# Splitting v of both PEER layers into bf16 halves beside the heads of the first mixer, and forming the expert outputs from the halves

## The reference

```python
    def block(args):
        xb, ib, gb = args
        hb = jax.nn.gelu(jnp.einsum('tkd,td->tk', u[ib], xb), approximate=False)
        return jnp.einsum('tk,tkd->td', gb * hb, v[ib])
```

## Time and profile before

| | us |
|---|---|
| median of 3 runs (lowest, highest) | 4829.14 (4827.85, 4833.03) |
| the profiled execution, its own time | 4834.75 |
| its span, first to last instruction | 4833.2 |

### The profile page before, as it was taken

The page is one execution under the profiler, slowest core; times in us unless marked ns, Lnnn a source line. Parts: engine busy times, 40 slices in busy tenths (PEclk is TensorE's granted clock), DMA queues, the critical chain, the costliest instruction groups (busy, mean ns, idle before and its releaser), DMA issues. The chain is left out here.

```text
span 4833.2 us, 54964 instructions
## 1 busy us (share of the span) xinstructions
PE 4347.5 (90%) x19374; PEld 2496.9 (52%) x19374; DVE 3212.7 (66%) x6400; ACT 1013.2 (21%) x1581; POOL 720.5 (15%) x548
## 2 busy tenths in 40 slices
PE   8999998978979989999998877987878998999998
PEld 5767674645545545544444555554444554444443
DVE  1666642679978767765653675469997886766664
ACT  2111101122224431100001253213333441100000
POOL 0000000002221113232210000001221112332220
PEclk9999999989989999999999999999998999999999
DMA  4111131149877779999992000116776779999995
GB/s 146 39 39 44 37 133 55 55 182 350 324 278 267 294 275 375 370 385 394 384 360 70 31 1 31 47 50 242 282 284 234 284 272 353 364 397 400 400 396 196
DMA packets 291813, 1101.75 MB, mean 228 GB/s; under 512 B 30704, under 2 KB 131184, under 8 KB 222576
## 3 DMA queue, kind: packets, MB, share of 16 engines
q0 software_dynamic: 74752, 539.00, 28.3%
q1 hardware_dynamic: 185136, 470.64, 27.2%
q10 hardware_dynamic: 31680, 88.88, 4.8%
HBM read 1005.61 MB, written 92.80 MB: 227 GB/s over the span
## 5 line engine op out<-in xcount | busy, mean ns | idle before, releaser
L774 POOL DMA_INDIRECT room_p<-in_uv,ga_eidx_p x512 | 702.8, 1373 | 3309.5 <-DVEq L801 2105.0
L1324 PE MATMUL ex_psF_p<-ex_vst_p,ex_gh_p 128*128 128x512 f32 x1920 | 851.5, 599 | 34.3 <-DVE ex_gh_p L1405 18.1
L800 DVE SCALAR_TENSOR_TENSOR ga_acc_p<-room_p,ga_gw_p,ga_acc_p 128x1024 f32<-128x1024 f32 x504 | 625.1, 1282 | 21.8 <-issue 1.7
L1324 PEld LDWEIGHTS ex_psF_p<-ex_vst_p,ex_gh_p 128*128 128x128 f32 x1920 | 365.9, 192 | 482.5 <-issue 460.6
L786 DVE CUSTOM_DVE_ANT_0 room_p<-room_p,hx_p 128x1024 f32<-128x1024 f32 x512 | 605.5, 1220 | 4.0 <-issue 4.0
L891 PE MATMUL eh_psH_sl_p<-h_hi_p,eh_uhi_sl_p 128*128 128x384 bf16 x1056 | 367.6, 348 | 160.0 <-DVE eh_ulo_sl_p L855 159.9
L1324 PE MATMUL ex_psF_p<-ex_ust_p,ex_gh_p 128*128 128x512 f32 x1152 | 502.1, 593 | 6.6 <-DVE ex_gh_p L1405 6.5
L1405 DVE TENSOR_TENSOR ex_gh_p<-ex_est_p,ex_gst_p 128x384 f32<-128x384 f32 x196 | 107.3, 558 | 397.7 <-DMA ex_est_p<-hidden 253.3
L891 PE MATMUL eh_psH_sl_p<-h_lo_p,eh_uhi_sl_p 128*128 128x384 bf16 x1056 | 366.3, 347 | 0.0
L1324 PEld LDWEIGHTS ex_psF_p<-ex_ust_p,ex_gh_p 128*128 128x128 f32 x1152 | 217.7, 190 | 286.6 <-issue 285.4
L891 PE MATMUL eh_psH_sl_p<-h_hi_p,eh_ulo_sl_p 128*128 128x384 bf16 x1056 | 365.4, 346 | 0.0
(11 more groups left out here) (248 smaller groups left out, 6275.5 us busy)
## 6 DMA issues: line engine op xcount, KB each, us to landing
ex_vst_p<-in_uv SPq DMA_DIRECT2D x160, 512.0 KB, 8.4
eh_ust_sl_p<-in_uT SPq DMA_DIRECT2D x132, 512.0 KB, 5.4
gates<-gt_gs_p ACTq DMA_DIRECT2D x24, 2048.0 KB, 8.0
ex_gst_p<-gates SPq DMA_DIRECT2D x128, 384.0 KB, 13.0
ex_ust_p<-in_uv SPq DMA_DIRECT2D x96, 512.0 KB, 9.3
ex_est_p<-hidden SPq DMA_DIRECT2D x196, 192.0 KB, 10.2
eh_ust_gt_p<-in_uT SPq DMA_DIRECT2D x64, 512.0 KB, 6.6
ex_ust_p<-in_uT SPq DMA_DIRECT2D x60, 512.0 KB, 8.8
```

Of the source, the lines that this page charges most:

```text
L774: self.nc.gpsimd.indirect_dma_start(self.slot[s % self.RING], None, self.uv, bass.IndirectOffsetOnAxis(self.eidx[:, s:s + 1], 0)).then_inc ...
L800: nc.vector.scalar_tensor_tensor(acc[:], row, self.gw[:, s:s + 1], acc[:], op0=ALU.mult, op1=ALU.add)
L1324: last = nc.tensor.matmul(psF[:, t, x, :], gh[n % 3][:, P * t:P * t + P], vbuf[vslot[n]][:, BANK * x:BANK * x + BANK], start=(n == 0), sto ...
```

## The change

In the first mixer, 32 blocks (`VSPLIT`) are handled beside each head, 16 of layer 0 and 16 of layer 1, so 256 in all, which is all of v. A block is 128 experts by 1024. POOL loads it in f32 (512 KB) into one of two buffers `vraw`; ScalarE copies it to bf16 (`high`), in four groups of eight ahead of the evacuations of the next head's projections, and for the last head four ahead of each of the eight modulation groups; VectorE subtracts that to get the low half (`low`), two blocks behind each of the 16 steps; POOL stores both halves together (512 KB) to a DRAM tensor `halves` and then issues the load after next. The two buffers of each kind are freed by the store's completion (`v_free`) and by the low half (`v_low`).

In both expert stages v is loaded as the two halves, into the same buffers and with as many bytes. The gated values are split as well, on ScalarE (`high`) and VectorE (`low`), with four buffers of each half, and a tile's output is formed from three bf16 products: high by high, high by low, low by high. The two row buffers of the modulation become one.

```diff
@@ rec_mixer
+        vraw = [sb(f"rec_vraw{i}", [P, D]) for i in range(2)]
+        vhl = [sb(f"rec_vhl{i}", [P, 2, D], BF16) for i in range(2)]
...
+            def fetch(h, j):
+                pool.dma_start(vraw[j % 2][:], rows_in[j // 16][h, j % 16, :, D:2 * D]).then_inc(v_in[j % 2], 16)
+
+            def stored(h, j):
+                pool.wait_ge(v_out[j % 2], 16 * (VSPLIT // 2 * h + j // 2) + 16)
+                pool.sem_inc(v_free, 1)
+
+            def split_rows(h, nxt):
+                for j in range(VSPLIT):
+                    pool.wait_ge(v_low, VSPLIT * h + j + 1)
+                    pool.sem_inc(v_seen, 1)
+                    pool.dma_start(halves[j // 16][h, j % 16], vhl[j % 2][:]).then_inc(v_out[j % 2], 16)
+                    if j + 2 < VSPLIT:
+                        fetch(h, j + 2)
+                    elif nxt is not None:
+                        fetch(nxt, j + 2 - VSPLIT)
+                    if j > 0:
+                        stored(h, j - 1)
+                stored(h, VSPLIT - 1)
+
             load(0)
+            fetch(0, 0)
+            fetch(0, 1)
             with pool.Fori(1, RH) as h:
+                split_rows(h - 1, h)
                 store(h - 1)
...
+            def high(h, js):
+                for j in js:
+                    act.wait_ge(v_in[j % 2], 16 * (VSPLIT // 2 * h + j // 2) + 16)
+                    act.wait_ge(v_free, VSPLIT * h + j + 1)
+                    nc.scalar.activation(vhl[j % 2][:, 0, :], vraw[j % 2][:], ACT.Copy).then_inc(v_high, 1)
...
-                evacuate(h, s, [Q_, FF_, FB_, G_])
+                for n in (Q_, FF_, FB_, G_):
+                    high(h - 1, range(VSPLIT * n // 4, VSPLIT * (n + 1) // 4))
+                    evacuate(h, s, [n])
...
             for g in range(later.groups):
+                high(RH - 1, range(VSPLIT * g // later.groups, VSPLIT * (g + 1) // later.groups))
...
+            def low(h, n):
+                for j in range(VSPLIT * (n - 1) // 16, VSPLIT * n // 16):
+                    dve.wait_ge(v_high, VSPLIT * h + j + 1)
+                    nc.vector.tensor_tensor(vhl[j % 2][:, 1, :], vraw[j % 2][:], vhl[j % 2][:, 0, :],
+                                            ALU.subtract).then_inc(v_low, 1)
...
                     take(h, n - 1)
+                    low(h, n)
@@ peer_experts
+        GH = 4 if halves is not None else 3
...
+                if halves is not None:
+                    sp.dma_start(vbuf[vslot[n]].bitcast(BF16), halves[n]).then_inc(v_in[vslot[n]], 16)
...
+            def output_halves(n):
+                pe.wait_ge(v_in[vslot[n]], 16 * vturn[n] + 16)
+                pe.wait_ge(g_low, n + 1)
+                both = vbuf[vslot[n]].bitcast(BF16)
+                for t in range(ND):
+                    tok = slice(P * t, P * t + P)
+                    for j, (g, v0) in enumerate(((g_hi[n % GH], 0), (g_hi[n % GH], D), (g_lo[n % GH], 0))):
+                        for x in range(2):
+                            last = nc.tensor.matmul(psF[:, t, x, :], g[:, tok], both[:, v0 + BANK * x:v0 + BANK * x + BANK],
+                                                    start=(n == 0 and j == 0), stop=(n == NK - 1 and j == 2))
+                last.then_inc(added, 1)
...
+            def high(n):
+                act.wait_ge(gated, n + 1)
+                if n >= GH:
+                    act.wait_ge(added, n - GH + 1)
+                nc.scalar.activation(g_hi[n % GH][:], gh[n % 3][:], ACT.Copy).then_inc(g_high, 1)
+
             for n in range(NK):
+                if halves is not None:
+                    high(n)
                 gelu(n + 1)
...
+            def low(n):
+                dve.wait_ge(g_high, n + 1)
+                nc.vector.tensor_tensor(g_lo[n % GH][:], gh[n % 3][:], g_hi[n % GH][:], ALU.subtract).then_inc(g_low, 1)
...
                 if n >= 3:
-                    dve.wait_ge(added, n - 2)
+                    dve.wait_ge(added if halves is None else g_low, n - 2)
...
                 take_u(n + 3)
+                while halves is not None and lows < (n + 1 if n < late or n == NK - 1 else n):
+                    low(lows)
+                    lows += 1
@@ kernel
+        halves = [nc.dram_tensor(f"halves{l}", [RH, 16, P, 2, D], BF16, kind="Internal").ap() for l in range(2)]
```

More of the change, by code:

```diff
@@ L222, in rec_mixer @@
         adab = sb("rec_adab", [P, NMOD * KD, 2])
-        rows = [sb(f"rec_rows{i}", [2, 2, BANK]) for i in range(2)]
+        rows = sb("rec_rows", [2, 2, BANK])
         wst = sb("rec_wst", [P, 5, KD, P])
@@ L568, in head @@
                 for d in range(2):
+                    low(h, 15 + d)
                     n = TR0 + d
@@ L1218, in _, with peer_experts @@
                 sp.wait_ge(sv[s], 16 * (NBL // 2))
-def peer_experts(nc, cst, modT, uT, uv, gates, hid, gather, late, h_hi, h_lo, tag):
+def peer_experts(nc, cst, modT, uT, uv, halves, gates, hid, gather, late, h_hi, h_lo, tag):
     J, TB = 8, 32
@@ L1317, in hidden @@
                 hidden_products(nc, psH[:, n % 2, 0:TD], u_hi[n % 3], u_lo[n % 3], h_hi, h_lo).then_inc(made, 1)
+            def output_halves(n):
[9 more added lines that the diff above has]
+                last.then_inc(added, 1)
             def output(n):
+                if halves is not None:
+                    return output_halves(n)
                 pe.wait_ge(v_in[vslot[n]], 16 * vturn[n] + 16)
@@ L1422, in _, with peer @@
             dve.drain()
-def peer(nc, cst, modT, wqk, uT, uv, gates, hid, tag, ada=None):
+def peer(nc, cst, modT, wqk, uT, uv, halves, gates, hid, tag, ada=None):
     tiles, pairs = (60, (2, 2, 3)) if ada else (72, (2, 1, 3))
@@ L1440, in peer @@
         peer_gates(nc, cst, pk, gates, gather, (uT, h_hi, h_lo, hid, late + tiles), tag)
-        peer_experts(nc, cst, modT, uT, uv, gates, hid, gather, late, h_hi, h_lo, tag)
+        peer_experts(nc, cst, modT, uT, uv, halves, gates, hid, gather, late, h_hi, h_lo, tag)
 NQ, NKV = AH * HD // P, AKV * HD // P
@@ L1845, in _ @@
             runs(dve, one)
+VSPLIT = 32
 class Const:
@@ L1865, in program @@
         cst.normw = normw[0]
+        halves = [nc.dram_tensor(f"halves{l}", [RH, 16, P, 2, D], BF16, kind="Internal").ap() for l in range(2)]
+        by_block = [v.rearrange("h j p e d -> (h j) p (e d)") for v in halves]
         with ExitStack() as c1:
@@ L1870, in program @@
                       {"cond": a["cond"], "xT": a["xT"], "ident": a["ident"], "iota": a["iota"], "normw": a["normw"],
-                       "normw_sb": normw})
+                       "normw_sb": normw},
+                      [a[f"uv{l}"].rearrange("(h j p) d -> h j p d", p=P, j=16) for l in range(2)], halves)
             out_projection(nc, cst, a["rec_w_out"], yT, mods[0], "_rec")
```

22 lines of the change are left out of this document (16 added, 6 removed).

## The result

| us | before | after |
|---|---|---|
| median (4 runs each) | 4830.32 | 5593.99 |
| lowest, highest | 4827.85, 4833.03 | 5583.95, 5604.63 |
| span of the profiled execution | 4833.2 | 5596.1 |

The changed kernel takes 1.1581 times as long, 95% interval 1.1557 to 1.1605: 764 us more. Forecast were 5266 and a range up to 5450, so the sign was right and the size too small: 437 us of the 764.

The account below looks back on a forecast made before the run. It took TensorE to bound the mixer, and TensorE and DMA together the expert stages. The profiled 4834.75 + 502 - 65 = 5272, stated as 5266 us for the median; forecast 5110 to 5400, range 5090 to 5450.

Parts of the forecast that it names:

- Term 2: First mixer: splitting v beside the heads lengthens their steps, +502 us, bounds +388 to +754.
- ring of 7.5: Mixer: store issue, next load, its landing, high half and low half follow in a closed loop, 7.5 us a step.
- rival A: Mixer: store, load and weights meet in the queues, loop 8.6 to 9.6 us, total 5400 to 5520; chance 0.15.
- VectorE's floor: Mixer: VectorE's own work plus two subtractions make a step at least 4.90 us.
- Term 1: Expert stages: bf16 output matmuls spare TensorE time, but bytes stay; -65 us, bounds -20 to -105.
- the DMA ceiling: Expert stages: transfers go no faster than 405 GB/s, so a late tile's 1.97 MB take 4.86 us.
- the new wait: Expert stages: TensorE's output waits for the gated values' low half, up to 0.3 us on 60 early tiles, 18 us.
- B: Mixer: TensorE falls to its lower clock, +124 us, total 5390; chance 0.10.
- C: Mixer: transfers are hidden, VectorE bounds steps of 4.9 to 5.8 us, total 4955 to 5065; chance 0.12.
- D: Expert stages: 405 GB/s is no limit, they gain 320 us; mixer steps fall to 4.9, total 4699; chance 0.02.
- The signs it gave: Mixer: steps 7.5 us, landing 4 to 4.5, DMA about 280 GB/s; expert stages some 45 and 20 us shorter.
- would make it wrong: Mixer steps near 5 us, an expert stage shorter by over 100 us, or stages that grow by the new wait.

Follow-up runs that it names:

- all three edits: Only the bf16 expert stages, against the kernel before: low half ahead of u's, at once in late tiles, awaited only before the last 6 matmuls; -24.9 us, ratio 0.9952.

## Why the prediction was wrong

**Term 2, the mixer: right in kind, mis-sized (+502 forecast, +740 measured).** The waits are those it named, VectorE's for ScalarE and, for three quarters of it, ScalarE's for the load. Its ring of 7.5 was 9.0 in a plain step and 9.36 over a head. Two terms were too small. The load, from the start of its issue: 0.55 + 3.3 + 0.75 = 4.60 forecast, 5.28 measured; POOL's wake: "some 0.1 for the semaphore", 0.76 measured. The first was short by more than it looks: the row's 3.3 runs from the start of an issue, so the forecast counted the load's 0.55 twice, and the landing itself, 3.3 + 0.75, was 1.2 too low. The rest lies in the first interval of a head, 12.7 where 7.5 was taken for it as for the others, and in the last head, whose step is 10.7. The step that failed is the choice inside the bounds: 5.4 for the landing was there, with +754, and was set aside "because 5.4 was measured beside gathers of 1 MB", and rival A because of "12% load in the mixer before". But the load that counts is the one after the change, and the change itself brings it to a DMA share of 0.66 to 0.69. Only the store ahead on the same queue was priced; the run with the stores on SyncE's queue shows that the place on the queue was not it.

**What stood behind the ring was not named.** Where the load is taken out (four buffers), the release through POOL is next, at 8.4, then the store's landing, at 8.1. The forecast listed the store's completion as freeing a buffer, but did not follow it through POOL's list, where it stands behind the next store and load.

**VectorE's floor** was near: 4.90 forecast, 5.18 measured without transfers, +190 against +229.

**Term 1, the expert stages: the DMA ceiling was right, the new wait was mis-sized (-65 forecast, +25 in the changed kernel).** With the low half formed at once the late tiles give 37 and 23 us, 60 together, where the forecast had 22 + 19 and 19, also 60. That is not luck alone: with all three edits stage 1's late tiles run at the ceiling while gathers last, 384 us for 80 tiles or 4.8 each at 403 GB/s, where 4.86 was forecast.

```profile
2122.00:2506.00 384.00, 325.58 (x1398) 138.23 (x1399) 281.31 (x435) 48.84 (x118) 92.14 (x80) 0.95 1.03 403
```

The step that failed is the bound of the wait, "up to 0.3 us on 60 tiles, 18 us of the 38", with the sentence that the small splits "lie beside the DMA time". The low half cost 39 us in the early tiles and held back 39 in the late ones, where it was not looked for. In the early tiles the forecast took VectorE as 23 to 28 of 40 us busy and left out its wait for ScalarE; with it, VectorE's list was as long as the tile, and its new operation came on top. In the late tiles the low half was priced by the operation's length, and in an in-order list it costs what stands ahead: the next tile's load (up to 10.84).

**Rivals.** A is what happened in the mixer, with a step in its range of 8.6 to 9.6; its 5400 to 5520 still carried the -65, so the 5594 lies above it. B's clock came (0.78), but its price did not: some 4 us at the heads' ends, and in the steps TensorE was not waited for. C needed transfers that land a microsecond sooner; they landed two later. D is refuted: with all three edits TensorE has gaps in the late tiles at 404 and 406 GB/s, and half the gathers' bytes make these tiles shorter.

**The signs it gave.** Steps of COPY_PREDICATED at 7.5: 9.4 in the mean. Landing 4 to 4.5: 5.3. DMA 280 GB/s: 217. Expert stages 45 and 20 shorter: 5 shorter and 23 longer by the table above. Of what "would make it wrong" it had the last: stages that grow by the new wait.

## What to carry to other kernels

Price a transfer's landing at the load of the DMA engines that the change makes, not the one it finds, and for a ring of few buffers take it from a row measured beside as much traffic. A new small operation costs what stands ahead of it in its engine's order, waits for loads included, so place it and the consumer's wait before pricing it. Count an engine's waits for its own helpers as part of its list: VectorE was busy for 26.8 of 40 us and yet had no room. Where a wait is removed, follow the buffer's release instruction by instruction: the next chain may be only 0.3 to 1 us shorter.

## What the runs showed of the hardware

A load of 512 KB lands in 3.3 us on SyncE's queue with little beside it, in 3.9 on POOL's with the other loads and no stores (a DMA share of 0.44 to 0.46 in the inner heads), and in 5.3 to 5.5 with as many stores beside it, at a DMA share of only 0.65 to 0.7 and about 215 to 235 GB/s. The Trainium skill ("DMA: Bandwidth & Descriptors", section "Anatomy of one DMA — SWDGE (gpsimd) path") gives 2.0 us and the bytes at 436 GB/s, an estimate of 3.2 us for 512 KB; the runs come near it only on SyncE's queue in a nearly idle mixer (3.3), and POOL's loads took longer in every run (medians of 3.9 to 6.2, beside more traffic). POOL issued its transfer 0.76 us behind the end of the VectorE instruction it waited for.
